# Two transformer blocks on one NeuronCore: last gate tiles, mixer sums and an output projection placed elsewhere in TensorE's order

## The reference, cut to what matters

```python
# first block, per layer
u = rms_norm(h, norm_g); z = u @ w_in
oa = forgetting_attention(qa, ka, va, log_f) * silu(ga)      # 8 heads of 64
ob = dilated_attention(rope(qb), rope(kb), vb) * silu(gb)    # 8 heads of 64
h = h + concat(oa, ob) @ w_out
h = h + (p_i @ w_ple) * sigmoid(rms_norm(h) @ w_ple_gate)

# second block, per layer
x = x + 0.5 * swiglu(rmsnorm(x), w1, w3, w2)                 # 2816 wide
q, f, i, g, u_b = split(rmsnorm(x) @ w_in)
o_a = hgrn2(q, f, i) normed * silu(g)                        # 4 heads of 128, gated recurrence
o_b = multiscale_pool(u_b)
x = x + concat(o_a, o_b) @ w_out
x = x + softmax(q k^T) v @ wo                                # 4 heads of 256 over 256 memory rows
x = x + 0.5 * swiglu(rmsnorm(x), w1, w3, w2)
```

## Time and profile before

| | us |
|---|---|
| median of 3 runs | 3117.42 |
| lowest, highest | 3112.37, 3121.12 |
| the profiled execution's own time | 3123.16 |
| its span, first to last instruction | 3121.3 |
| TensorE busy in it | 3050.1 (98%) |
| VectorE, ScalarE busy | 1641.3, 1104.7 |
| mean granted TensorE clock | 0.986 of full |

### The profile page before, as it was taken

How to read it: one execution, slowest core, us unless ns; L and a number is a source line. 1 busy time by engine, 2 the same in 40 slices (tenths; PEclk the granted TensorE clock), 3 DMA queues, 4 the chain that set the end, 5 groups by cost and what they waited for, 6 DMA issues and landing times.

```text
span 3121.3 us, 33738 instructions
## 1 busy us (share of the span) xinstructions
PE 3050.1 (98%) x14426; PEld 2516.5 (81%) x14426; DVE 1641.3 (53%) x1870; ACT 1104.7 (35%) x1312; POOL 67.3 (2%) x70
## 2 busy tenths in 40 slices
PE   8999999999999999999999999999999999999998
PEld 6788877878888888888788888888888788788886
DVE  4455554555554557364455445645455463544545
ACT  5344444444422226333332222422235333432222
POOL 0000000000000000110000000000000200000000
PEclk9899999999999999999999999999999999999999
DMA  4110222102223223103222222222232014222221
GB/s 142 50 68 28 102 82 68 64 32 102 95 102 110 95 94 118 58 28 116 100 95 95 95 95 94 95 95 95 95 121 95 28 60 139 71 95 95 95 95 68
DMA packets 41493, 270.56 MB, mean 87 GB/s; under 512 B 5728, under 2 KB 5984, under 8 KB 9984
## 3 DMA queue, kind: packets, MB, share of 16 engines
q1 hardware_dynamic: 41344, 268.40, 24.7%
HBM read 266.22 MB, written 2.10 MB: 86 GB/s over the span
## 4 chain that ended last, share of the span: by engine, by line
PE 82%; DVE 10%; ACT 6%; issue 1%; DVEq 1%; DMA 0%; SPq 0%; ACTq 0%
PE PS L216 23%; PE PS L218 23%; PE PS L217 23%; DVE w_lo L201 4%; ACT w_hi L193 3%; PE PS L962 2%; PE PS L602 2%; DVE XT L1197 2%; PE PS L951 1%; PE PS L1708 1%; PE PS L1943 1%; PE PS L1969 1%; PE PS L1690 1%; DVE E L1619 1%; DVE total L280 0%
## 5 line engine op out<-in xcount | busy, mean ns | idle before, releaser
L193 ACT ACTIVATE w_hi<-w_raw 128x2048 fp32r<-128x2048 f32 x242 | 463.2, 1914 | 1202.8 <-PE PS L218 1198.8
L201 DVE TENSOR_TENSOR w_lo<-w_raw,w_hi 128x2048 fp32r<-128x2048 f32 x242 | 554.8, 2292 | 411.7 <-ACT w_hi L193 410.8
L216 PE MATMUL PS<-uh_b,w_hi 128*128 128x512 f32 x1312 | 512.2, 390 | 0.0
L218 PE MATMUL PS<-uh_b,w_lo 128*128 128x512 f32 x1312 | 511.1, 390 | 0.0
L217 PE MATMUL PS<-ul_b,w_hi 128*128 128x512 f32 x1312 | 510.9, 389 | 0.0
L216 PE MATMUL PS<-w_hi,uh_a 128*128 128x512 f32 x768 | 305.3, 398 | 14.4 <-DVE ul_a L271 10.9
L216 PE MATMUL PS<-uh_a,w_hi 128*128 128x512 f32 x800 | 313.7, 392 | 3.2 <-DVE ul_a L518 2.2
L218 PE MATMUL PS<-uh_a,w_lo 128*128 128x512 f32 x800 | 311.7, 390 | 0.0
L217 PE MATMUL PS<-ul_a,w_hi 128*128 128x512 f32 x800 | 311.6, 390 | 0.0
L217 PE MATMUL PS<-w_lo,uh_a 128*128 128x512 f32 x768 | 300.7, 392 | 0.0
L218 PE MATMUL PS<-w_hi,ul_a 128*128 128x512 f32 x768 | 300.3, 391 | 0.0
(11 more groups left out here) (294 smaller groups left out, 3786.8 us busy)
## 6 DMA issues: line engine op xcount, KB each, us to landing
w_raw<-in_weights SPq DMA_DIRECT2D x242, 1024.0 KB, 4.9
XT<-in_xT SPq DMA_DIRECT2D x8, 256.0 KB, 9.0
mem_raw<-in_mem SPq DMA_DIRECT2D x2, 1024.0 KB, 4.8
out<-XT SPq DMA_DIRECT2D x8, 256.0 KB, 2.0
bands<-in_bands SPq DMA_DIRECT2D x2, 768.0 KB, 6.4
mask_numbers<-in_masks SPq DMA_DIRECT2D x1, 1152.0 KB, 7.2
p_raw<-in_pT SPq DMA_DIRECT2D x2, 512.0 KB, 3.5
lb<-in_lb_logits SPq DMA_DIRECT2D x2, 512.0 KB, 5.8
```

What stands on the lines that cost most here:

```text
L193: act.activation(self.hi[g % 2][:], self.raw[g % 2][:], ACT.Copy).then_inc(self.hi_done.sem, 1)
L201: dve.tensor_tensor(self.lo[g % 2][:], self.raw[g % 2][:], self.hi[g % 2][:], ALU.subtract).then_inc(self.lo_done.sem, 1)
L216: pe.matmul(out, sh, mh, start=first, stop=False)
L218: return pe.matmul(out, sl, mh, start=False, stop=last)
```

## The change

In the attention starts, the gate projection's tiles 0 and 1 stay ahead of the attention; tile 2 comes behind the scores of head 1, tile 3 behind the transposes of head 0. ScalarE's Silu of tiles 2 and 3 stands behind the exponentials of head 1. Each tile has its own signals. VectorE waits for all four only ahead of the first head that it finishes.

In the mixer, head 0's key transposes and sums come ahead of the chunk decays and the outer products, which move to banks 4 and 5 to 7; head 0 uses the other buffer `E`. VectorE takes the states after it has weighed head 0, and signals each. The key transposes of head h+2 come ahead of the outputs of head h.

In the attention to the memory, the transposes of heads 2 and 3 go to banks 0, 1 and 2, 3, and behind each of them TensorE makes two of the eight feature steps of the output projection's block 0. The rest of the diff renames semaphores.

```diff
@@ Residual
+    def begin(self, pe, c):
+        assert c == self.begun
+        self.begun += 1
+        if c == 0:
+            self.k.w.ready(pe, self.g0)
+        self.u_ready(pe, c)
+        for f in range(2):
+            i = split_products(pe, self.bank(f), self.k.w.part(self.g0, c * 256 + f * P, P), [x[:, c, :] for x in self.u],
+                               c == 0, c == KD - 1)
+        if c == KD - 1:
+            i.then_inc(self.k.w.used.sem, 1)
@@ Residual.tensor
-        for b in range(1 if self.turn else 0, 4):
+        started = self.turn or self.begun
+        for c in range(self.begun, KD if self.begun else 0):
+            self.begin(pe, c)
+        for b in range(1 if started else 0, 4):
@@ HeadsProjection.scalar
-        w.wait_used(act, g0 + 7)
-        for t in range(NT):
-            i = act.activation(m.G[:, t, :], rows_of(4, t), ACT.Silu, scale=k.rt[:, t:t + 1])
-        i.then_inc(self.g_out.sem, 1)
+        for t in range(2):
+            self.take_gates(act, t)
@@ HeadsProjection.tensor
-        project(3, 1, 4)
+        w.ready(pe, g0 + 7)
+        for t in range(2):
+            self.last_gates(pe, t)
+
+    def last_gates(self, pe, t):
+        for c in range(4, KD):
+            i = split_products(pe, self.k.PS[:, 4 + t, :], [x[:, c, t * P:(t + 1) * P] for x in self.u],
+                               self.k.w.part(self.g0 + 7, (c - 4) * 512, 512), False, c == KD - 1)
+        i.then_inc((self.g_done if t < NT - 1 else self.k.w.used).sem, 1)
@@ HeadsAttention.scalar
+            if h == 0:
+                self.proj.take_gates(act, 2)
+                self.proj.take_gates(act, 3)
@@ HeadsAttention.vector
-        dve.wait_ge(*self.g_out.at(1))
...
+            if h == 1:
+                dve.wait_ge(*self.proj.g_out.at(NT))
             if h >= 1:
                 finish(h - 1)
@@ HeadsAttention.tensor
             if h == 0:
-                pe.wait_ge(*self.g_out.at(1))
+                self.proj.last_gates(pe, 2)
+                pe.wait_ge(*self.proj.g_out.at(2))
...
             turn(h)
+            if h == 0:
+                self.proj.last_gates(pe, 3)
+            if 1 <= h <= 2:
+                pe.wait_ge(*self.proj.g_out.at(2 + h))
             if h >= 1:
                 outputs(h - 1)
@@ Recurrence.vector
         weigh(0)
+        self.states.take_states(dve)
@@ Recurrence.scalar
         exps(0)
+        self.states.take_decays(act)
         exps(1)
@@ Recurrence.tensor
+        turn_keys(0)
         pe.wait_ge(*self.states.mapped_read.at(4))
         sums(0)
+        pe.wait_ge(*self.kcopied.at(1))
+        self.states.decays(pe)
+        self.states.states(pe)
+        turn_keys(1)
         sums(1)
         for h in range(HH):
             scores(h)
+            if h + 2 < HH:
+                turn_keys(h + 2)
@@ CrossAttention
+    BANKS = (4, 4, 0, 2)
@@ CrossAttention.tensor
             if h + 2 < XH:
                 self.scores(pe, h + 2)
+            else:
+                pe.wait_ge(*self.ptact.at(2))
+                pe.wait_ge(*self.ptdve.at(2))
+                for c in (2 * h - 4, 2 * h - 3):
+                    self.follower.begin(pe, c)
```

More of the change, by code:

```diff
@@ L636, in __init__ @@
         self.even_copied, self.odd_copied, self.v_out = sig("heads_even_copied", 2), sig("heads_odd_copied", 2), sig("heads_v_out", NT)
-        self.g_out, self.rows_set = sig("heads_g_out", 1), sig("heads_rows_set", 1 if dilated else 2)
+        self.g_done = sig("heads_g_done", NT - 1)
+        self.g_out, self.rows_set = sig("heads_g_out", NT), sig("heads_rows_set", 1 if dilated else 2)
         if not dilated:
@@ L1511, in vector, with take_states @@
                .then_inc(self.mapped_read.sem, 1)
+        for c in range(NT - 1):
+            dve.wait_ge(*self.suffix_exp.at(c + 1))
+            dve.tensor_tensor(m.Kp[:, c, :], m.Kp[:, c, :], m.K[:, c, :], ALU.mult).then_inc(self.kp.sem, 1)
+    def take_states(self, dve):
+        k, m = self.k, self.m
         dve.wait_ge(*self.outer.at(1))
         dve.wait_ge(*self.dec_exp.at(1))
-        dve.tensor_copy(m.St[:, 0, :], k.PS[:, 4, :]).then_inc(self.state_read.sem, 1)
+        dve.tensor_copy(m.St[:, 0, :], k.PS[:, 5, :]).then_inc(self.state_read.sem, 1)
         for c in (1, 2):
@@ L1536, in tensor, with decays @@
             pe.matmul(k.PS[:, 4 + c, :], uh[:, 6, 0:P], ul[:, c, :], start=False, stop=True).then_inc(self.suffix.sem, 1)
-        pe.wait_ge(*self.suffix_exp.at(4))
+    def decays(self, pe):
+        k, m = self.k, self.m
         for c in (1, 2):
@@ L1578, in gpsimd @@
             for n in range(LEVELS):
-                e = right(m.E[h % 2][:, n, :], n, 0)
+                e = right(m.E[(h + 1) % 2][:, n, :], n, 0)
                 pool.tensor_tensor(e, e, right(m.Kf[h % 2][:], n, 0), ALU.mult).then_inc(self.keysweighed.sem, 1)
@@ L1675, in tensor, with turn_keys @@
         k, m, right, (uh, ul) = self.k, self.m, self.right, self.u
-        def sums(h):
-            if h:
+        def turn_keys(h):
+            if h == 0:
+                pe.wait_ge(*self.states.suffix_exp.at(1))
+            elif h == 1:
+                pe.wait_ge(*self.states.dec_exp.at(1))
+            else:
                 pe.wait_ge(*self.kcopied.at(h))
-            else:
-                pe.wait_ge(*self.states.state_read.at(1))
             for c in range(NT):
@@ L1684, in sums @@
             i.then_inc(self.kturned.sem, 1)
+        def sums(h):
             for c in range(NT):
@@ L1694, in scores @@
         def scores(h):
-            W = m.E[h % 2]
+            W = m.E[(h + 1) % 2]
             for unit in range(self.UNITS):
                 pe.wait_ge(*self.weighed.at(self.UNITS * h + unit + 1))
+                if h == 0 and unit < 2:
+                    pe.wait_ge(*self.states.state_read.at(unit + 1))
                 pe.wait_ge(*self.keysweighed.at(LEVELS * h + min(2 * unit + 2, LEVELS)))
@@ L1718, in outputs @@
                 pe.wait_ge(*self.outread.at(h))
+            else:
+                pe.wait_ge(*self.states.state_read.at(NT - 1))
             cols = slice(h * P, (h + 1) * P)
@@ L2161, in two_models @@
             fox.follower = proj
-            dil = HeadsAttention(sig, k, m1, scores, NH * HEAD, proj.g_out)
+            dil = HeadsAttention(sig, k, m1, scores, NH * HEAD, proj)
             turn = dil.turning = Turn(sig, k, m1.mix, k.UA, dil)
```

62 lines of the change are left out of this document (36 added, 26 removed).

## The result

The changed kernel takes 3068.22 us (median of 4 runs, 3067.20 to 3070.07), against 3114.89 us for the kernel of before in runs beside it (4 runs, 3109.17 to 3121.12). The ratio is 0.985, 95% interval 0.983 to 0.987. The forecast was 3077 us with a range of 3065 to 3100.

A forecast was written before the change was run, and what follows sets the result against it. TensorE, busy for 98%, was taken as the bound, with its gaps and low-clock stretches left to win. 8.2 + 17.5 + 4.0 + 3.3 + 4.4 + 8.1 = 45.5 us off 3123.16 gave 3077 us, range 3065 to 3100.

The forecast's parts named there:

- the forecast's case: The whole kernel gets faster by the summed terms, to 3077 us; chance 0.74.
- Attention starts, gaps: Four attention starts: gate products fill TensorE's gaps, gaining 2.05 us a start, 8.2 in all; bounds 0 and 2.8 a start.
- Attention starts, clock: Layers 0 and 1, forgetting attention: the clock's falls of 23.7 and 13.5 us go, gaining 17.5 us.
- Mixer: Both layers' mixers: gaps gain 4.0 us, the clock's first fall 3.3 and its second 4.4.
- I take this fall as gone in one layer of the two: Mixer, head 0's scores: the clock's second fall goes in one layer only, gaining 4.4 us.
- a few tenths of gap remain: Mixer, head 0's scores: the 1.1 us wait ahead of the third unit shrinks to a few tenths.
- the time returns one step later: Mixer, heads 2 and 3: moving key transposes, 0.4 us each, gains nothing, since the sums then run into ScalarE.
- Memory: Attention to the memory: waits for the copies go, 6.5 us, and a clock fall, 1.6; together 8.1, bounds 6.5 and 8.4.
- the prediction's list of falls: Low-clock stretches read from the first profile: in two forgetting attentions, the mixers and once at the memory's 2.03 us gap.
- Rival 1: Whole kernel: only the gaps go, the clock falls as often because of narrow matmuls; 3104 us, chance 0.11.
- Rival 2: Attention starts: ScalarE bounds heads 0 to 2, table loads cost 2.56 us a start; 3085 or some 3091 us, chance 0.08.
- Rival 3: Attention starts: a remaining gap lowers the clock and it stays low, 31 us an attention; slower than before, chance 0.03.

The follow-up runs named there:

- e4: The kernel of before, unchanged, run for a second profile; 3109.59 us in its one run.
- e6: The changed kernel with one exponential and one Silu more (two table loads) on ScalarE behind tile 3's Silu in each attention start; 3104.05 us.
- e9: The changed kernel with the mixer's chunk decays ahead of the suffix sums and the unread fourth suffix sum and its exponential left out; 3071.41 us.
- e10: The kernel of e9 with the pooled map's sixteen transposes split, eight ahead of head 2's outputs and eight ahead of head 3's; 3075.20 us.
- e11: The kernel of e10 with VectorE taking the states ahead of weighing head 0; 3063.94 us.
- e1: The changed kernel with the gate projection, the Silu and the first heads in the order of before; 3085.25 us.
- e5: The changed kernel with two more 128x256 copies on ScalarE behind tile 3's Silu in each attention start, results unused; 3068.48 us.
- e7: The changed kernel with the key transposes of the mixer's heads 2 and 3 behind the outputs again; 3070.56 us.
- e8: The changed kernel with VectorE taking the states ahead of weighing head 0, as before the change; 3067.52 us.

## Why the prediction was right

The result lies 9 us under the forecast, inside its range, and the forecast's case is the one that happened. Term by term, forecast against the two traces:

- *Attention starts, gaps*: 8.2 us forecast. The two starts that had fallen in neither trace gained 2.07 us each (46.6 against 44.5 us from head 0's scores to head 7's), forecast 2.05. The two waits that are left are 0.29 and 0.23 us, forecast 0.35 and 0.4; that the total is met to 0.02 us is in part chance.
- *Attention starts, clock*: 17.5 forecast. The two starts that had fallen gained 13.7 and 8.1 us, less 2.07 each 17.7. The size goes with the execution that was profiled: in e4 the four starts had only 3.2 us each at the low clock. That the gaps cause the falls was argued there. e6 shows that a gap of 3 us does, with nothing else moved, and in the mixer a gap of 1.6 us did so in one layer of the two in e9's and e10's profiles, and e11, without the gap, has no such fall in head 0. For the gaps of up to 1.16 us, e1 brings them back together with falls in three starts, but it also takes the wide products from among the narrow ones, and these two weren't parted; e5's 0.62 us with the products in place brought no fall.
- *Mixer*: 4.0 + 3.3 + 4.4 = 11.7 forecast, 17.7 measured. This term was mis-sized. By the low stretches (13.6 us in layer 0 and 17.0 in layer 1 before, none and 6.8 with the change) some 11.5 us of it are clock and 6.2 gaps, where 7.7 and 4.0 were forecast. Three steps of it failed. "I take this fall as gone in one layer of the two" was wrong, head 0's fall is gone in both, 4.4 us more; two falls of 3.4 us that layer 1 still had, elsewhere in its mixer, take some of it back. "a few tenths of gap remain" in head 0's scores was wrong, none does. The reason is when VectorE's masks begin, 3.64 us behind the start of the scores before the change (1319.38) and 2.26 with it (1288.03), where the third unit of the scores, which needs the first mask, is due some 3.7 us behind the start. The rows of the first masks, before and with the change:

```profile
1323.02 0.94 DVE L1635 COPY_PREDICATED AT<-masks,PS 128x256 f32<-128x256 uint8 x2
...
1290.29 0.96 DVE L1689 COPY_PREDICATED AT<-masks,PS 128x256 f32<-128x256 uint8 x2
```

  Before, the weighing of head 0 stood right ahead of the masks and ended at 1323.09. And "the time returns one step later" for the key transposes was wrong, they are worth 0.39 us a head (e7).
- *Memory*: 8.1 forecast, 8.9 measured: each wait carried some 0.2 us that its row doesn't show.
- The rest, 1.7 us in the opening, is a low stretch of 3.4 us from 28.0 on that the prediction's list of falls left out. It comes and goes with the execution (it is there in the profiles of e1, e4 and e7).

The level was right for a reason worth noting. The profiled execution was 5.7 us slower than the median, and the prediction read that as falls of the clock, hence didn't take it off twice. e4 bears it out: 13.6 us less with the same waits. The clock fell in all four starts of e4, where no gap is longer than 1.16 us (0.35, 0.70 and 1.16 us, among narrow matmuls). The rule that the clock falls after a long idle gap (the Trainium skill, TensorE: Matmul & The Clock Gate, "Why this matters for your kernels") does not account for these falls. It agrees with e6, whose longer gap of 3.0 us brought the clock down in all four, and for longer.

Rival 1, that the clock falls as often, is out by the change's own trace: 1.00 in all four attentions, 6.8 us low in the mixers where it was 30.6. Rival 2 was right in its mechanism, ScalarE is late at head 0's outputs and head 2's transposes, and wrong in size, 0.29 + 0.23 us a start where it had 2.56. Rival 3 did not happen here, and its price was of the right kind: it had 31 us an attention, and the worst of e6 lost 21.6 us, with 47.6 us at the low clock.

## What to carry to other kernels

Where TensorE is busy for 98%, read the granted clock behind each of its gaps before pricing the gap: between the two profiled executions 21 us of gaps carried 34 us of clock, and behind the same gap among short matmuls the clock cost 1.7 us in one execution and 12 in the other (first attention, e4 and the first profile). Such a gap can be filled with wide matmuls that are ready, even ones that come from the next stage. And when an edit brings TensorE somewhere earlier, look at what is ready there with nothing to spare: e9 took 3 us of gaps and work out of TensorE's way, got them back as a wait for VectorE and lost 3 us. And where TensorE waits for several semaphores, look in the code which ones they are: the view named the weighing, and it was the copy behind it.

## What was not expected of the hardware

Once low, the clock stayed low for up to 47.6 us, of which TensorE was busy for 46.5, without idle time behind the gap, in its float32 head work (e6). It came back in the midst of the same work, with narrow matmuls before and behind; in e4 it was back within 3.4 us in the same work. What decides between the two was not tried.

That VectorE is slower beside GpSimd was in the prediction; that the slowing goes both ways was not: 5.77 against 2.43 us for seven float32 steps on VectorE, and 6.44 against 5.09 on GpSimd (the change against e8).
